# Differential attention outputs by token rows, with one root for all heads and a memory block moved ahead of the odd output projection

## What is computed

```
o_h = (softmax(q1 k1^T / 8) - lambda * softmax(q2 k2^T / 8)) v_h      256 tokens x 128
y_h = o_h / sqrt(mean(o_h^2 over the 128) + 1e-5) * g * (1 - lambda_init)
mix = concat(y_0 ... y_7) @ odd_w_out                                 256 x 1024
x   = layer_norm(alpha * x + mix)
```

## Time and profile before

| | |
|---|---|
| median of 3 runs | 2639.06 us (2637.83 to 2645.97) |
| profiled execution, its own time | 2637.99 us |
| its span in the profile | 2636.2 us |
| PE busy | 2217.9 us, 84% |
| DVE, ACT, POOL busy | 765.8, 615.9, 743.3 us |

### The profile page before, as it was taken

The page is one execution under the profiler, slowest core; times in us unless marked ns, Lnnn a source line. Parts: engine busy times, 40 slices in busy tenths (PEclk is TensorE's granted clock), DMA queues, the critical chain, the costliest instruction groups (busy, mean ns, idle before and its releaser), DMA issues.

```text
span 2636.2 us, 31029 instructions
## 1 busy us (share of the span) xinstructions
PE 2217.9 (84%) x12038; PEld 1414.0 (54%) x12038; DVE 765.8 (29%) x1446; ACT 615.9 (23%) x884; POOL 743.3 (28%) x625
## 2 busy tenths in 40 slices
PE   7988889989698899979799999999979876565665
PEld 6866778878486789735454544444447532121211
DVE  4744220122721311146353122222146530000001
ACT  3544323433533234211241000000021410000000
POOL 7746346887163567710200000000010100000000
PEclk9989989989699899979799899999999787877787
DMA  8324668644046487441101699999973039999996
GB/s 259 128 96 144 224 207 278 228 153 159 32 145 220 149 286 270 169 147 68 64 1 64 250 422 422 422 422 422 421 284 116 30 137 422 421 421 422 422 421 281
DMA packets 171520, 635.91 MB, mean 241 GB/s; under 512 B 10040, under 2 KB 16440, under 8 KB 122120
## 3 DMA queue, kind: packets, MB, share of 16 engines
q1 hardware_dynamic: 168368, 623.79, 61.4%
q0 software_dynamic: 2880, 10.29, 1.5%
q10 hardware_dynamic: 152, 0.17, 0.0%
HBM read 633.17 MB, written 1.05 MB: 241 GB/s over the span
## 4 chain that ended last, share of the span: by engine, by line
PE 65%; DMA 17%; DVE 8%; ACT 3%; issue 3%; POOL 2%; SPq 1%; DVEq 0%; ACTq 0%
PE bank L1107 14%; PE bank L505 9%; PE bank L507 9%; PE bank L506 9%; DMA ring<-in_w_up 7%; PE bank L943 5%; DMA ring<-in_w_gate 4%; DMA ring<-in_w_down 3%; PE bank L1063 3%; PE bank L1121 3%; PE bank L1131 2%; PE bank L679 2%; POOL ring_r L1264 2%; PE bank L952 2%; DMA ring<-in_ffn_w_gu 2%
## 5 line engine op out<-in xcount | busy, mean ns | idle before, releaser
L1264 POOL TENSOR_TENSOR ring_r<-ring,ring_r 128x512 fp32r<-128x512 f32 (+1 forms) x544 | 671.9, 1274 | 411.3 <-ACT ring_r L1361 350.4
L1107 PE MATMUL bank<-ring,arena 128*64 128x512 f32 (+1 forms) x3072 | 587.8, 706 | 191.5 <-DMA ring<-in_w_up 65.3
L505 PE MATMUL bank<-ring_r 128*128 128x256 f32 (+1 forms) x1504 | 471.7, 314 | 51.2 <-DVEq L1823 27.4
L1107 PEld LDWEIGHTS bank<-ring,arena 128*64 128x64 f32 (+1 forms) x3072 | 175.7, 140 | 586.2 <-issue 572.6
L507 PE MATMUL bank<-xT_r,ring_r 128*128 128x256 f32 x1248 | 359.4, 288 | 0.0
L506 PE MATMUL bank<-ring_r 128*128 128x256 f32 x1248 | 358.0, 287 | 0.0
L1361 ACT ACTIVATE ring_r<-ring 128x2048 fp32r<-128x2048 f32 (+1 forms) x138 | 253.1, 1840 | 424.2 <-PE bank L507 230.2
L505 PEld LDWEIGHTS bank<-ring_r 128*128 128x128 f32 x1504 | 295.5, 196 | 78.0 <-DVEq L1823 30.0
L507 PEld LDWEIGHTS bank<-xT_r,ring_r 128*128 128x128 f32 x1248 | 245.1, 196 | 0.0
L506 PEld LDWEIGHTS bank<-ring_r 128*128 128x128 f32 x1248 | 244.2, 196 | 0.9 <-issue 0.7
L1294 POOL TENSOR_TENSOR arena<-const 128x1024 f32<-128x1024 f32 x6 | 12.4, 2072 | 734.9 <-DVEq L1823 622.6
(11 more groups left out here) (298 smaller groups left out, 2573.3 us busy)
## 6 DMA issues: line engine op xcount, KB each, us to landing
ring<-in_w_gate SPq DMA_DIRECT2D x128, 1024.0 KB, 17.0
ring<-in_w_up SPq DMA_DIRECT2D x128, 1024.0 KB, 18.7
ring<-in_w_down SPq DMA_DIRECT2D x128, 1024.0 KB, 18.9
ring<-in_ada_w SPq DMA_DIRECT2D x48, 1024.0 KB, 6.2
ring<-in_ffn_w_gu SPq DMA_DIRECT2D x40, 1024.0 KB, 5.3
ring<-in_ffn_w_down SPq DMA_DIRECT2D x20, 1024.0 KB, 5.0
ring<-in_mem_wkv SPq DMA_DIRECT2D x16, 1024.0 KB, 5.2
ring<-in_w_in SPq DMA_DIRECT2D x16, 1024.0 KB, 14.2
```

The source lines that it names most:

```text
L505: pe.matmul(dst, w_hi, v_hi, start=first, stop=False)
L1107: mm = pe.matmul(dst[nb][W * j:W * j + W, :], src[:, 2 * q + c, W * j:W * j + W], wide_of((u0 + k) % RING)[:, c, UN * nb:UN * nb + UN], st ...
L1264: pool.tensor_tensor(lo[:, c], whole[:, c], hi_of(u)[:, c, 0:n], ALU.subtract).then_inc(*signal("w_lo", (u, c)))
```

## The change

The output of a head is computed by token rows (tokens on the partitions) and not transposed, so the sum of squares runs along the row. DVE copies it into `o_rows`, ACT squares 128x128 pieces with an accumulated sum, one value for each token and head. One root and one reciprocal over 128x16 serve all heads. DVE scales the rows in four instructions, PE turns them (16 transposes of 128x128, in two groups of eight, one for each tile of 128 tokens), and the factor g is applied as the hi and lo parts are taken out of the bank. The ones-matmul goes. Memory block 0 is loaded, split and multiplied ahead of `odd_out`; between its two halves and behind it stand the two groups of transposes. `odd_out` waits for its input for each tile of tokens and not for all of it.

```diff
 # weight_plan
             matrix(("odd_in",), w["odd_w_in"][0])
+            block(("mem_kv", layer, 0), w["mem_wkv"][layer], 0, UN)
             matrix(("odd_out",), w["odd_w_out"][0])
...
-            matrix(("mem_kv", layer), w["mem_wkv"][layer])
+            for b in range(1, 4):
+                block(("mem_kv", layer, b), w["mem_wkv"][layer], UN * b, UN * b + UN)
 # TensorE
                 for t in range(T2):
+                    if tile_ready:
+                        tile_ready(t)
                     for h in (n_units - 2, n_units - 1):
...
-                    def square_sums(u):
-                        pe.wait_ge(*after("ssq", u["n"]))
-                        b = open_bank(("ss", u["n"]), u["n"] % 2)
-                        pe.matmul(b[:, 0:SEQ], con("ones"), raw[:, u["n"] % 2, :], start=True, stop=True)\
-                          .then_inc(*filled_now(("ss", u["n"])))
+                    def value_rows(u):
+                        pe.wait_ge(*after("probsT", u["key"]))
+                        b = open_bank(("o",) + u["key"], (7, 1)[u["n"] % 2])
+                        for t in range(T2):
+                            for kb in range(2):
+                                mm = pe.matmul(b[:, P * t:P * t + P], probsT_of(u)[:, kb, P * t:P * t + P], u["v"][kb],
+                                               start=(kb == 0), stop=(kb == 1))
+                        mm.then_inc(*filled_now(("o",) + u["key"]))
+
+                    def turn_o(t):
+                        for g in range(2):
+                            pe.wait_ge(*after("oT", ("o_norm", g, t)))
+                            b = dense_bank(("oT", g, t))
+                            for h in range(4):
+                                mm = pe.transpose(b[:, P * h:P * h + P], o_rows[:, t, 512 * g + P * h:512 * g + P * h + P], ident)
+                            mm.then_inc(*filled_now(("oT", g, t)))
-                    for i in range(C_HEADS + 2):
+                    for i in range(C_HEADS + 1):
                         if i + 2 < C_HEADS:
                             diff_scores(diff_units[i + 2])
                         if i < C_HEADS:
                             turn(diff_units[i])
-                        if i >= 2:
-                            square_sums(diff_units[i - 2])
-                        if 0 <= i - 1 < C_HEADS:
-                            values(diff_units[i - 1])
-                    pe.wait_ge(*after("y_lo", ("diff", C_HEADS - 1)))
-                    out_proj(("odd_out",))
+                        if i:
+                            value_rows(diff_units[i - 1])
+                    memory = project_T_halves(("mem_kv", layer, 0), m_parts, new_bank=side_bank)
+                    for t in range(T2):
+                        next(memory)
+                        turn_o(t)
+                    out_proj(("odd_out",), tile_ready=lambda t: pe.wait_ge(*after("y_lo", (1, t))))
 # ScalarE
-                            diff_out(diff_units[i - 2])
+                            o_squares(diff_units[i - 3])      # two Square of 128x128 with accum_out, from o_rows
...
-                    act.activation(dvar, dvar, ACT.Sqrt).then_inc(*signal("rstd", "diff"))
-                    for h in range(C_HEADS):
-                        act.wait_ge(*after("oT", ("diff", h)))
-                        act.activation(x_hi[:, h], y1T[:, h, :], ACT.Copy).then_inc(*signal("y_hi", ("diff", h)))
+                    act.activation(o_std, o_var, ACT.Sqrt).then_inc(*signal("rstd", "diff"))
+                    for t in range(T2):
+                        for g in range(2):
+                            act.wait_ge(*full(("oT", g, t)))
+                            act.activation(x_hi[:, 4 * g:4 * g + 4, P * t:P * t + P], bank_of(("oT", g, t))[:, :].rearrange("p (a b) -> p a b", a=4),
+                                           ACT.Copy, scale=lam[:, 6:7]).then_inc(*signal("y_hi", (g, t)))
+                    evac_memory(layer, 0)
 # VectorE
-                            dve.wait_ge(*full(("ss", i - 2)))
-                            link(dve.tensor_scalar(dvar[:, i - 2, :], bank_of(("ss", i - 2))[:, 0:SEQ], 1.0 / P, LN_EPS, ALU.mult, ALU.add))
-                            drop(("ss", i - 2))
-                            link(dve.reciprocal(dvar[:, i - 2, :], dvar[:, i - 2, :]))
+                            key = ("o",) + diff_units[i - 2]["key"]
+                            dve.wait_ge(*full(key))
+                            at = P * (i - 2)
+                            link(dve.tensor_copy(o_rows[:, :, at:at + P], bank_of(key)[:, 0:SEQ].rearrange("p (t d) -> p t d", t=T2)))
+                            drop(key)
+                            done("oT", ("o_rows", i - 2))
+                    dve.wait_ge(*after("ssq", C_HEADS - 1))
+                    dve.tensor_scalar(o_var, o_ssq, 1.0 / P, LN_EPS, ALU.mult, ALU.add).then_inc(*signal("var", "diff"))
                     dve.wait_ge(*after("rstd", "diff"))
-                    for h in range(C_HEADS):
-                        y = y1T[:, h, :]
-                        dve.scalar_tensor_tensor(y, y, lam[:, 6:7], dvar[:, h, :], ALU.mult, ALU.mult)\
-                           .then_inc(*signal("oT", ("diff", h)))
-                    for h in range(C_HEADS):
-                        dve.wait_ge(*after("y_hi", ("diff", h)))
-                        dve.tensor_tensor(y1_lo[:, h], y1T[:, h, :], x_hi[:, h], ALU.subtract).then_inc(*signal("y_lo", ("diff", h)))
+                    link(dve.reciprocal(o_rstd, o_std))
+                    for t in range(T2):
+                        for g in range(2):
+                            rows = o_rows[:, t, 512 * g:512 * g + 512].rearrange("p (h d) -> p h d", h=4)
+                            dve.tensor_tensor(rows, rows, o_rstd[:, t, 4 * g:4 * g + 4].unsqueeze(2).to_broadcast([P, 4, P]), ALU.mult)\
+                               .then_inc(*signal("oT", ("o_norm", g, t)))
+                    for t in range(T2):
+                        for g in range(2):
+                            dve.wait_ge(*after("y_hi", (g, t)))
+                            at = (slice(None), slice(4 * g, 4 * g + 4), slice(P * t, P * t + P))
+                            key = ("oT", g, t)
+                            link(dve.scalar_tensor_tensor(y1_lo[at], bank_of(key)[:, :].rearrange("p (a b) -> p a b", a=4), lam[:, 6:7], x_hi[at],
+                                                          ALU.mult, ALU.subtract))
+                            drop(key)
+                            done("y_lo", (g, t))
```

More of the change, by code:

```diff
@@ L274, in build @@
         lam_raw = area(7680, 4, 64)
-        dvar = area(6144, C_HEADS, SEQ)
+        o_rows = area(6144, T2, D)
         gate_w = area(2304, KC, 16)
@@ L280, in build @@
         gcols = sb("gcols", [P, 2, 2, 2, 4])
+        o_ssq, o_var, o_std, o_rstd = (aff[:, :, 0, C_HEADS * i:C_HEADS * i + C_HEADS] for i in range(4))
         g_row = area(4096, 2, D)
@@ L561, in project_rows_halves, with project_rows @@
                 yield
-            def project_rows(key, src, kc=KC, new_bank=dense_bank, ready=None):
+            def project_rows(key, src, kc=KC, new_bank=dense_bank, ready=None, tile_ready=None):
                 out_banks = [new_bank(key + ("out", t)) for t in range(T2)]
@@ L768, in _, with out_proj @@
             pe.wait_ge(*after("oT", ("na", B_HEADS - 1)))
-            def out_proj(key, kc=KC, src=y_parts, ready=None):
+            def out_proj(key, kc=KC, src=y_parts, ready=None, tile_ready=None):
                 for nb in range(2):
-                    project_rows(key + (nb,), src, kc, ready=ready if nb == 0 else None)
+                    project_rows(key + (nb,), src, kc, ready=ready if nb == 0 else None, tile_ready=tile_ready if nb == 0 else None)
             def norm_T(i):
@@ L847, in _ @@
                             turn(diff_units[i])
-                        if i >= 2:
-                            square_sums(diff_units[i - 2])
-                        if 0 <= i - 1 < C_HEADS:
-                            values(diff_units[i - 1])
-                    pe.wait_ge(*after("y_lo", ("diff", C_HEADS - 1)))
-                    out_proj(("odd_out",))
+                        if i:
[5 more added lines that the diff above has]
+                    out_proj(("odd_out",), tile_ready=lambda t: pe.wait_ge(*after("y_lo", (1, t))))
                 n0 = 3 * layer
                 if layer == 1:
-                    for b in range(2):
-                        project_T(("mem_kv", layer, b), m_parts, new_bank=side_bank)
+                    project_T(("mem_kv", layer, 1), m_parts, new_bank=side_bank)
                 for b in range(2 + (layer == 0), 4):
@@ L1573, in diff_exps @@
                         done("probs_exp", u["key"])
[L1575 to L1584, removed]
@@ L1585, in _, with o_squares @@
-                    for i in range(C_HEADS + 2):
+                    def o_squares(u):
+                        h = u["n"]
```

(20 more changed lines are left out.)

1 line of the change is left out of this document (removed).

## The result

The changed kernel takes 2611.74 us (median of 4 runs, 2607.21 to 2614.08), the kernel before 2640.85 in the same comparison (2637.83 to 2645.97): a ratio of 0.9887, with a 95% interval of 0.9869 to 0.9906. So it is faster, by 29 us.

The account below looks back on a forecast made before the run. The prediction took PE as mostly the bound, with two holes: a head loop paced by DVE and a serial tail. Gains of 7.35 + 14.0 = 21.4 us gave 2617.5 us, range 2612 to 2627.

Parts of the forecast that it names:

- Part 1, the loop: Differential heads: period falls to 4.6 us, set by ACT and DVE together; five periods gain 7.35 us (4.9 to 9.0).
- ACT's pair of squares: In each head: two ACT squares of 128x128 with a sum each, taken at 1.1 us for the pair.
- Part 2, the tail: From the eighth head's start through odd_out and the memory blocks: 14.0 us gained (8.5 to 16).
- I take 5 us low: First half of the moved block: PE's clock stays low for 5 us, so the half takes 8.0 us.
- The two large terms: Behind odd_out's start: 11.5 us of block work already done, and 2.9 us from odd_out starting at full clock.
- The new chain: Tail: copy, squares, table load, root, reciprocal, scaling covered by the half block, 3.1 us to spare, 0.9 at full clock.
- rival C: odd_out's weight splits come late, POOL being behind: PE stops up to 6.9 us once or twice; chance 0.1.
- the residual norm: Behind odd_out: hidden behind three memory blocks (34.5 us) instead of four, still free.
- Rival A: Heads: the loop gains nothing and stays near 6 us, only the tail counts, 2625 us; chance 0.12.
- D: odd_out and memory blocks: PE stays at the low clock far into them, kernel slower, up to 2666 us; chance 0.03.
- Rival B: Tail: the clock falls behind each group of transposes, losing 3 us, 2620.5 us; chance 0.1.
- The forecast's bounds: Whole kernel: upper gains of 9.0 us in the loop and 16 us in the tail, the latter with full clock at once.

Follow-up runs that it names:

- r3: The changed kernel once more, unchanged, for its third profile, timed beside a further version with memory products in the heads: 2611.91 us, ratio 0.9906.
- e6: The changed kernel, but odd_out waits for both token tiles before its first product: 2613.81 us, ratio 0.9904.
- r1: The kernel before once more, unchanged, for a second profile: 2635.71 us.
- e3: The changed kernel with two useless DVE instructions of 128x256 behind the output copy of five heads: 2621.92 us, ratio 0.9932.
- e4: The changed kernel with both halves of the moved memory block first and both groups of transposes behind them: 2611.98 us, ratio 0.9896.
- e1: The changed kernel with memory block 0 back behind odd_out: 2617.27 us, ratio 0.9925.
- e2: The kernel before with only memory block 0 moved ahead of odd_out, computed whole: 2625.55 us, ratio 0.9956.

## Why the prediction was right in direction and too small

**Part 1, the loop: right mechanism, 2.0 us too small** (9.4 for 7.35). DVE was named as bound before and after; with ACT the forecast took 4.6 a head. ACT's pair of squares came to 0.8 where 1.1 was taken, so ACT did not set the pace of the first four periods, and they took 17.60 us, 4.40 each; that is 0.8 of the 2.0. The other 1.2 is a mistake in counting: the forecast multiplied five equal periods, but the seventh head has no maxima behind it any more, and its period is 3.36 us (697.95 to 701.31), with 1.01 of waiting for ACT in it. Before, that one was short as well (5.55, 701.90 to 707.45), but the average over five hid it.

**Part 2, the tail: the term that failed is the clock.** "I take 5 us low" was the step. None of the profiles has that: in nine of them, with the block at this place, it began at full clock or reached it in 0.7 us (r3). That is 2.3 us of the error (8.0 forecast for the half block, 5.71 measured). The values were taken at 1.9 us each, as at the low level; in the first profile the block began 4.50 us behind the eighth head's start and not 6.85: another 2.35. Where the values ran at the low level and the block followed them (e6, r3), it began 6.25 us behind that start, so 1.75 of the 2.35 is the clock, and the other 0.6 comes from adding up durations that overlap. The transposes took 0.79 for 0.95, twice. Together 5.0: odd_out started at 17.5 and not at 22.5. The two large terms were right, 11.5 + 2.9 = 14.4 against 14.33, but the 2.9 with some luck: it rests on 6.2 us at the low level in the one profile, and r1 had 3.0 there, worth 1.4.

**Why it was wrong.** The forecast took the level of a stretch (0.50 from 708 to 720) from one execution as a property of the code. The runs show two things in its place. The values part really goes either way from one execution to the next: high in the changed kernel's first two profiles and in e3 and e4, low in e1, e6 and r3. The idle time ahead of the last turning is 1.8 us in the first, and 1.8, 1.15 and 1.7 in these three. The block part is regular in these nine profiles: full clock from its first product or 0.7 us later, whatever the level of the heads. Between the last turning and the block PE was never idle for more than 0.9 us at a time; that this is the reason is not shown. The quicker pace is not the reason (e3). The kernel before was low at this place in both of its profiles and in the first half of it in e2, and why it stays low there more often is not settled; it has gaps of 0.9 us between values and ones-matmuls that the changed kernel lacks, but no run took those alone.

**What was free was free.** The new chain was covered: scaled rows of the first tile at about 710.6 (two of the four in 2.50 us from 709.33), the transposes due at 711.5, so 0.9 us to spare, the figure given for full clock. POOL's first chunk was begun 3.0 us behind odd_out's start and POOL released no odd_out matmul: rival C did not happen. Three memory blocks hid the residual norm. Rival A and D did not happen. Rival B did not happen either: products right behind a group of transposes ran at full clock in every profile that has them there, e4 won nothing by moving the transposes behind the block, and in e1 the clock rose during sixteen transposes. Only e6 fell behind a group, and there a wait of 2.48 us stood between. So the rule of the Trainium skill that it leaned on (TensorE: Matmul & The Clock Gate, Part 4: PE-mode transpose) brought no loss here: groups of eight transposes of 1.04 us between products did not lower the clock.

**The range.** The measured median lies 0.26 us below it. The forecast's bounds (loop 9.0, tail 16) gave 2614, and the range began at 2612; the miscounted period (1.2 us) and values at full clock were in no bound.

## What to carry to other kernels

Where PE waits for a serial chain of small steps, put a product there that depends on nothing, and put it between the steps of the chain, not only ahead of them (1.8 us of the stage in e4). Here the gain was that product's time at full clock, 11.5 us, plus the 1.4 to 2.9 us that the stretch behind it had lost at the low level. When one engine sets the pace of a loop, the others' gaps are room as well: 1.4 us of products in each head left the period at 4.36 us and made the stage 10.6 us shorter (97.9 for 108.5). And count periods one by one where the loop's ends leave steps out, and take the level of TensorE's clock in a half-idle stretch from more than one profile, or put both levels into the range.

## What the runs showed that I had not expected

The same instructions ran at 0.50 or at 1.00 in the last heads, 2 us of the stage apart. Idle time alone does not tell which comes: behind 1.8 us without work the last turning was high in the first profile and low in e1, behind 1.6 us odd_out was high (e4), and behind 2.5 us it began high and fell to 0.51 after 1.3 us (e6). Behind the longest stretches it was low each time, but not for the same time: the transposes behind 4.0 us (e1), and odd_out behind 10.5 us for 6.2 us or for 3.0. A reciprocal of 128x256 takes 1.75 us where a copy of that shape takes 0.42, and one of 128x16 takes 0.25, so the one reciprocal for all heads relieves the engine that sets the pace of 1.79 us a head, gap included. The ones-matmuls went from PE, which had gaps in the heads anyway; no run takes out the one without the other. The change of ACT's table cost no more than the load itself: 1.28 us, and the root began 0.02 us behind it.
